# Narrow products of two weight chunks issued after the wide products of both

## The chip, the cores and the metric

The kernel runs on one core of a Trainium2 chip. The metric is the device time of one execution in microseconds (us); a profile of one execution stands beside it. Engines are called by the profile's names: PE is TensorE's matmul, PEld its weight load, DVE VectorE, ACT ScalarE, POOL GpSimd, SPq the queue that issues the DMAs.

## The reference, cut to what matters

Two blocks, 256 tokens of width 2048, all in float32. First a hybrid layer (spatial gating, a state space branch, attention over a memory, gates, an output projection), then a convolution block and a squared-ReLU MLP. Most of the time goes into products of a 256-row activation with large weights:

```
proj = rms_norm(x, pre_g) @ w_in                     # 2048 x 13312
k, v = rms_norm(mem, mem_g) @ w_k, ... @ w_v
branch = einsum('bsnc,ncd->bsnd', ys, w_branch)      # three times 1024 x 2048
out = merged @ w_out                                 # 2048 x 2048
u = h @ w_pw1 + b_pw1 ... @ w_pw2 + b_pw2            # 2048 x 4096, 2048 x 2048
h = h + square(relu(rms_norm(h) @ w_up)) @ w_down    # 2048 x 8192, 8192 x 2048
```

The attention over the memory is `softmax(q @ k.T / 16) @ v` for four heads of 256; its softmax runs while other weights are multiplied.

## The kernel before

**Chunks.** All weights come from HBM in 686 chunks of 128 x 1024 floats (512 KB). `plan()` writes out the list `STEP`: for each chunk c the job j (one output tile) and the index i of the chunk within the job. In a job of kind "W" a chunk holds eight 128 x 128 weight tiles. A job with `nch` = 2 has two chunks (K = 2048), one with `nch` = 1 has one (K = 1024). Kinds "M" and "G" and "T" are other layouts; they are not touched.

**Split in two parts.** float32 products are done as three fp32r products. Each chunk lands in `raw`; ACT copies it to the rounded `wh` (L663, `high`); DVE (in a later stretch POOL) subtracts to get the remainder `wl` (L1042, `low`), which takes the place of `raw`. Activations stand as `hi` and `lo` too. A W chunk does eight products of 512 columns (`wh` times hi and lo at once, L1854; "wide" below) and then eight of 256 columns (`wl` times hi, L1859; "narrow"), all into one PSUM bank.

**What sets the order.** Every engine runs one program in order over c. PE at step c does first the small products that other branches need at that step (the norm's sums `mean_squares` L1908 and `norm_across` L1926, `softmax` with its transposes L1972 and its products with V L1981, the state space products L1937, L1947 and L1951), then `chunk(c)`. At the end of each chunk PE raises `s_mm`. ACT's step c begins with `high(c + 3)`, which waits for `s_mm` to be c (the slot of `wh`, `WN` = 4 of them, is free); DVE's step c begins with `low(c + 3)`, which waits for that copy. What ACT and DVE do else at step c stands behind these two, since the engines don't reorder. SP issues the load of chunk c + 6 once `s_mm` is c (`RAW` = 7 slots). PE waits for `s_hi` ahead of the wide products and for `s_low_v` ahead of the narrow ones. Results leave their bank after the job's last chunk (ACT L677, DVE L1087), and three or four jobs later the bank is used again.

**The places that the prediction speaks of.** Step 9: `mean_squares(1)`, whose sums DVE and ACT turn into a diagonal matrix `dg` (L1060, L667, L1062, L1524) in their step 9, for `norm_across(1)` at PE's step 10; steps 29 and 30: the same for the memory. Steps 112 to 159: `softmax(c)`. Steps 81 to 244: the state space products `bu` and `cy`. Step 328 (`POST`): the sums after the output projection, which PE waits for.

Of the kernel before, what the change touches and what calls it, by code (L numbers as in the profile page):

```python
# [15 lines left out]
T = 256  # L16
RAW, WN = 7, 4
# [149 lines left out]
STEP, JOBS = plan()  # L167
# [27 lines left out]
LOW_V, LOW_G, HIGH = {}, {}, {}  # L195
# [105 lines left out]
def _build(nc, a, out, ctx):  # L301
    def sem(name):
        return ctx.enter_context(nc.semaphore(name))
# [4 lines left out]
    def at(name, off, n, dt=F32):  # L308
        return nc.alloc_sbuf_tensor_at(name, [128, n], dt, offset=base + off)[:, :]
# [12 lines left out]
    wl = at("wl", o_raw, RAW * CH, F32R).rearrange("p (s n) -> p s n", s=RAW)  # L322
    wh = at("wh", o_wh, WN * CH, F32R).rearrange("p (s n) -> p s n", s=WN)
# [63 lines left out]
    bank = [ctx.enter_context(nc.psum_tensor(f"bank{i}", [128, 512], F32))[:, :] for i in range(8)]  # L387
# [53 lines left out]
    s_hi, s_low_v, s_low_g, s_mm = sem("s_hi"), sem("s_low_v"), sem("s_low_g"), sem("s_mm")  # L441
# [1354 lines left out]
    def tensor(e):  # L1796
        w = Waits(e)
# [9 lines left out]
        def low_there(c):  # L1807
            if c in ON_POOL:
                w.wait_ge(s_low_g, LOW_G[c])
            else:  # L1810
                w.wait_ge(s_low_v, LOW_V[c])

        def ready(per, k):
            return k // per + 1 if per else NORMED_FOR[k]

        def chunk(c):
            j, i = STEP[c]
            pair, s_act, per, n0 = ACTS.get(j.stage, (None,) * 4)
            n0 = j.t // 4 * 16 if j.stage == "dn" else n0
            if i == 0:  # L1820
                for before in j.before:
                    if before is not None and before.kind == "W":
                        w.wait_ge(s_comb, before.comb)
                    elif before is not None:
                        w.wait_ge(s_evac, before.evac)
            if j.kind == "C":
                taps(c, j)
                return
            s, r = c % WN, c % RAW
            first_part, last_part = i == 0, i == j.nch - 1  # L1830
            if j.kind != "W":
                low_there(c)
            if j.kind == "G":
                ins = chunk_for_all(j, i, s, r, pair, s_act, per)
            elif j.kind == "M":
                for kk in range(2):
                    k = 2 * i + kk
                    w.wait_ge(s_act, n0 + k // per + 1)
                    rh = wh[:, s, kk * 512:kk * 512 + 512]
                    rl = wl[:, r, kk * 512:kk * 512 + 512]  # L1840
                    for h in range(2):
                        xh = pair.hi[:, k, h * 128:h * 128 + 128]
                        xl = pair.lo[:, k, h * 128:h * 128 + 128]
                        dst = bank[j.banks[h]]
                        e.matmul(dst, xh, rh, start=first_part and kk == 0, stop=False)  # L1845
                        e.matmul(dst, xh, rl, start=False, stop=False)  # L1846
                        ins = e.matmul(dst, xl, rh, start=False, stop=last_part and kk == 1)  # L1847
            elif j.kind == "W":
                dst = bank[j.banks[0]]
                w.wait_ge(s_hi, HIGH[c])  # L1850
                for kk in range(8):
                    k = 8 * i + kk
                    w.wait_ge(s_act, n0 + ready(per, k))
                    e.matmul(dst.rearrange("p (h t) -> p h t", h=2), wh[:, s, kk * 128:kk * 128 + 128],  # L1854
                             pair.both[:, :, k, :], start=first_part and kk == 0, stop=last_part and kk == 7,
                             skip_group_check=True)
                low_there(c)
                for kk in range(8):
                    ins = e.matmul(dst[:, 0:T], wl[:, r, kk * 128:kk * 128 + 128], pair.hi[:, 8 * i + kk, :],  # L1859
                                   start=False, stop=last_part and kk == 7, skip_group_check=True)  # L1860
            else:
                dst = bank[j.banks[0]]
                for kk in range(8):
                    k = 8 * i + kk
                    w.wait_ge(s_act, n0 + ready(per, k))
                    lh = wh[:, s, kk * 128:kk * 128 + 128]
                    ll = wl[:, r, kk * 128:kk * 128 + 128]
                    e.matmul(dst[:, 0:T], lh, pair.hi[:, k, :], start=first_part and kk == 0, stop=False)  # L1868
                    e.matmul(dst[:, 0:T], lh, pair.lo[:, k, :], start=False, stop=False)  # L1869
                    ins = e.matmul(dst[:, 0:T], ll, pair.hi[:, k, :], start=False, stop=last_part and kk == 7)  # L1870
            ins.then_inc(s_mm, 1)

        def chunk_for_all(lead, i, s, r, pair, s_act, per):


            n = len(lead.members)
            for kk in range(lead.kpc):
                k = lead.kpc * i + kk
                w.wait_ge(s_act, ready(per, k))
                for m, j in enumerate(lead.members):  # L1880
                    if k == 0:
                        for before in j.before:
                            if before is not None and before.kind == "W":
                                w.wait_ge(s_comb, before.comb)
                            elif before is not None:
                                w.wait_ge(s_evac, before.evac)
                    o = (kk * n + m) * 128
                    lh, ll = wh[:, s, o:o + 128], wl[:, r, o:o + 128]
                    a, z = k == 0 and j.col == 0, k == 15
                    if j.kind == "W":  # L1890
                        both = bank[j.banks[0]]
                        e.matmul(both.rearrange("p (h t) -> p h t", h=2), lh, pair.both[:, :, k, :], start=a, stop=z,  # L1892
                                 skip_group_check=True)
                        ins = e.matmul(both[:, 0:T], ll, pair.hi[:, k, :], start=False, stop=z, skip_group_check=True)
                        if z and j.tells:
                            ins.then_inc(s_grp, 1)
                        continue
                    e.matmul(of(j), lh, pair.hi[:, k, :], start=a, stop=False, skip_group_check=True)  # L1898
                    e.matmul(of(j), lh, pair.lo[:, k, :], start=False, stop=False, skip_group_check=True)
                    ins = e.matmul(of(j), ll, pair.hi[:, k, :], start=False, stop=z, skip_group_check=True)  # L1900
                    if z and j.tells:
                        ins.then_inc(s_grp, 1)
            return ins
# [81 lines left out]
        def taps(c, j):  # L1985


            w.wait_ge(s_raw[c % RAW], 16 * (c // RAW + 1))
            w.wait_ge(s_shift[j.idx % 3], 64 * (j.idx // 3 + 1))
            for m in range(8):  # L1990
                for g in range(4):
                    n = 32 * (8 * g + m)
                    ins = e.matmul(bank[j.banks[0]][32 * g:32 * g + 32, 0:T], raw[:, c % RAW, n:n + 32],  # L1993
                                   shifted[j.idx][:, g, 4 * m:4 * m + T], start=m == 0, stop=m == 7)
            ins.then_inc(s_mm, 1)
# [29 lines left out]
        for c in range(NC):  # L2025
# [4 lines left out]
            if c in (BIAS + 1, BIAS + 3):  # L2030
                h = (c - BIAS) // 2
# [5 lines left out]
            if Z <= c < Z + 4 * Z_STEP and (c - Z) % Z_STEP == 0:  # L2037
                i = (c - Z) // Z_STEP
# [4 lines left out]
                for g in (2 * i, 2 * i + 1):  # L2043
                    for h in range(2):
                        o = 256 * (g % 2) + 128 * h
                        ins = e.matmul(bank[7][:, o:o + 128], vn[:, h, g * 128:g * 128 + 128], sgw[:, g, :], start=True,
                                       stop=True)
# [3 lines left out]
            if S5 <= c < S5 + 32 * S5_STEP:  # L2051
                n, i = divmod(c - S5, S5_STEP)
# [39 lines left out]
            if FFN + 6 <= c < FFN + 22 and (c - FFN) % 2 == 0:  # L2092
# [5 lines left out]
                for i in range(4):  # L2098
                    ins = e.transpose(bank[4 + n % 3][:, i * 128:i * 128 + 128],
                                      Xf[:, n // 2 * 4 + i, n % 2 * 128:n % 2 * 128 + 128], ident)  # L2100
                ins.then_inc(s_tx, 1)
            chunk(c)

    with nc.Block() as block:
        @block.sync
        def _(e):
            sync(e)

        @block.gpsimd
        def _(e):  # L2110
            gpsimd(e)

        @block.scalar
        def _(e):
            scalar(e)

        @block.vector
        def _(e):
            vector(e)

        @block.tensor
        def _(e):
            tensor(e)
# [81 lines left out]
```

## Time and profile before

| | |
|---|---|
| median of 3 runs | 2039.89 us (2036.79 to 2042.66) |
| the profiled execution | 2038.79 us, of which span 2037.0 us |
| PE busy | 1997.4 us (98%) |
| DVE busy | 1526.5 us (75%) |
| ACT busy | 984.8 us (48%) |
| POOL busy | 365.6 us (18%) |
| TensorE clock granted, mean | 0.992 |

The span reaches from the first to the last instruction; 1.8 us lie around it. Matmul ends are modelled and overlap the next start, so a busy PE need not be PE at its peak; the distance between starts is what a product costs.

### The profile page before, as it was taken

The numbers are of one execution on the slowest core, as the hardware profiler recorded it, in microseconds if no ns is written. First come the engines' busy times: TensorE is split into PE (matmuls) and PEld (weight loads), VectorE is DVE, ScalarE is ACT, GpSimd is POOL, SyncE is SP. The second block draws the span as 40 slices with busy tenths as digits, with TensorE's granted clock in tenths as the row PEclk, the third lists the DMA queues.
The fourth block names the chain that finished last, engine by engine and source line by source line (L and its number), as shares of the span: only waits on it lengthen the run. The fifth ranks groups of instructions, "written<-read, shape, count | busy, mean of one in ns | idle before, by whom it ended". The sixth has DMA issues, their size and how long they took to land.

```text
span 2037.0 us, 29904 instructions
## 1 busy us (share of the span) xinstructions
PE 1997.4 (98%) x11766; PEld 1735.0 (85%) x11766; DVE 1526.5 (75%) x2398; ACT 984.8 (48%) x1451; POOL 365.6 (18%) x276
## 2 busy tenths in 40 slices
PE   8999999999899999999999999999999999999997
PEld 7888888888788888888899978888888888888886
DVE  6877889887899986688899976776467557656754
ACT  6545454444444445557543446554344444434443
POOL 0000234333333410000287744000000000000000
PEclk9999999999999999999899999999999999999999
DMA  8655555445455555565456564555665666665553
GB/s 319 216 185 177 186 186 168 163 153 167 148 176 176 164 181 191 187 228 189 142 183 209 187 193 156 190 196 190 191 193 187 195 190 190 190 195 188 188 195 134
DMA packets 107132, 379.00 MB, mean 186 GB/s; under 512 B 12016, under 2 KB 15856, under 8 KB 106864
## 3 DMA queue, kind: packets, MB, share of 16 engines
q1 hardware_dynamic: 106992, 377.09, 57.6%
q8 instruction: 93, 1.52, 0.3%
q14 instruction: 47, 0.39, 0.1%
HBM read 374.06 MB, written 2.98 MB: 185 GB/s over the span
## 4 chain that ended last, share of the span: by engine, by line
PE 81%; DVE 13%; issue 3%; ACT 2%; DMA 1%; SPq 0%; DVEq 0%; ACTq 0%
PE bank L1854 34%; PE bank L1859 17%; PE bank L1845 7%; PE bank L1846 7%; PE bank L1847 7%; DVE wl L1042 3%; DVE bank L1607 3%; ACT wh L663 1%; PE bank L1868 1%; PE bank L1870 1%; PE bank L1869 1%; PE bank L1892 1%; DVE scr L1087 1%; PE bank L1993 1%; PE bank L1898 0%
## 5 line engine op out<-in xcount | busy, mean ns | idle before, releaser
L1042 DVE TENSOR_TENSOR wl<-raw,wh 128x1024 fp32r<-128x1024 f32 x610 | 760.6, 1251 | 370.8 <-ACT wh L663 368.8
L663 ACT ACTIVATE wh<-raw 128x1024 fp32r<-128x1024 f32 x680 | 712.4, 1055 | 543.3 <-PE bank L1847 226.8
L1854 PE MATMUL bank<-Hr,wh 128*128 128x512 f32 x2304 | 581.8, 394 | 1.3 <-ACT wh L663 0.9
L1854 PEld LDWEIGHTS bank<-Hr,wh 128*128 128x128 f32 x2304 | 415.1, 189 | 81.8 <-issue 5.9
L1854 PE MATMUL bank<-Yr,wh 128*128 128x512 f32 x1280 | 326.0, 397 | 15.4 <-ACT wh L663 8.5
L1859 PEld LDWEIGHTS bank<-Hr,wl 128*128 128x128 f32 x2304 | 314.2, 190 | 22.7
L1859 PE MATMUL bank<-Hr,wl 128*128 128x256 f32 x2304 | 321.1, 282 | 0.0
L1854 PEld LDWEIGHTS bank<-Yr,wh 128*128 128x128 f32 x1280 | 231.6, 190 | 60.4 <-ACT wh L663 8.5
L606 POOL TENSOR_TENSOR wl<-raw,wh 128x1024 fp32r<-128x1024 f32 x70 | 170.0, 2437 | 350.6 <-ACT wh L663 350.6
L1845 PE MATMUL bank<-wh,Yr 128*128 128x512 f32 x576 | 224.2, 389 | 0.0
L1846 PE MATMUL bank<-wl,Yr 128*128 128x512 f32 x576 | 224.1, 389 | 0.0
L1847 PE MATMUL bank<-wh,Yr 128*128 128x512 f32 x576 | 224.1, 389 | 0.0
L1859 PEld LDWEIGHTS bank<-Yr,wl 128*128 128x128 f32 x1280 | 176.0, 192 | 12.7
L1859 PE MATMUL bank<-Yr,wl 128*128 128x256 f32 x1280 | 179.6, 283 | 0.0
L1847 PEld LDWEIGHTS bank<-wh,Yr 128*128 128x128 f32 x576 | 108.1, 188 | 22.6
L1868 PE MATMUL bank<-Hr,wh 128*128 128x256 f32 x448 | 127.4, 284 | 0.0
L1845 PEld LDWEIGHTS bank<-wh,Yr 128*128 128x128 f32 x576 | 108.2, 188 | 22.2
L1846 PEld LDWEIGHTS bank<-wl,Yr 128*128 128x128 f32 x576 | 108.2, 188 | 22.1
L1869 PE MATMUL bank<-Hr,wh 128*128 128x256 f32 x448 | 126.8, 283 | 0.0
L1870 PE MATMUL bank<-Hr,wl 128*128 128x256 f32 x448 | 126.8, 283 | 0.0
L1607 DVE SCALAR_TENSOR_TENSOR bank<-upad,cst,bank 128x256 f32<-128x256 f32 x290 | 121.7, 479 | 2.3
L621 POOL TENSOR_TENSOR wcs<-tab 128x256 f32<-128x256 f32 x32 | 39.6, 1238 | 464.8 <-DVE turned_s L1408 303.5
(334 smaller groups left out, 1925.3 us busy)
## 6 DMA issues: line engine op xcount, KB each, us to landing
raw<-in_w_up SPq DMA_DIRECT2D x128, 512.0 KB, 4.1
raw<-in_w_dn SPq DMA_DIRECT2D x128, 512.0 KB, 4.2
raw<-in_w_g SPq DMA_DIRECT2D x96, 512.0 KB, 3.5
raw<-in_w_p SPq DMA_DIRECT2D x80, 512.0 KB, 3.5
raw<-in_w_b SPq DMA_DIRECT2D x48, 512.0 KB, 3.4
raw<-in_w_out SPq DMA_DIRECT2D x32, 512.0 KB, 3.5
raw<-in_w_bx SPq DMA_DIRECT2D x16, 512.0 KB, 6.3
raw<-in_w_q SPq DMA_DIRECT2D x16, 512.0 KB, 4.1
```

The costliest lines, as they stand in the source:

```text
L606: e.tensor_tensor(wl[:, c % RAW, :], raw[:, c % RAW, :], wh[:, c % WN, :].bitcast(F32), ALU.subtract).then_inc(s_low_g, 1)
L663: e.activation(wh[:, c % WN, :], raw[:, c % RAW, :], ACT.Copy).then_inc(s_hi, 1)
L1042: e.tensor_tensor(wl[:, c % RAW, :], raw[:, c % RAW, :], wh[:, c % WN, :].bitcast(F32), ALU.subtract).then_inc(s_low_v, 1)
L1607: e.scalar_tensor_tensor(ac, pad[:, j:j + T], wj, ac, ALU.mult, ALU.add).then_inc(s_v, w.own())
L1845: e.matmul(dst, xh, rh, start=first_part and kk == 0, stop=False)
L1846: e.matmul(dst, xh, rl, start=False, stop=False)
L1847: ins = e.matmul(dst, xl, rh, start=False, stop=last_part and kk == 1)
L1854: e.matmul(dst.rearrange("p (h t) -> p h t", h=2), wh[:, s, kk * 128:kk * 128 + 128], pair.both[:, :, k, :], start=first_part and kk == 0, ...
L1859: ins = e.matmul(dst[:, 0:T], wl[:, r, kk * 128:kk * 128 + 128], pair.hi[:, 8 * i + kk, :], start=False, stop=last_part and kk == 7, skip_ ...
L1868: e.matmul(dst[:, 0:T], lh, pair.hi[:, k, :], start=first_part and kk == 0, stop=False)
L1869: e.matmul(dst[:, 0:T], lh, pair.lo[:, k, :], start=False, stop=False)
L1870: ins = e.matmul(dst[:, 0:T], ll, pair.hi[:, k, :], start=False, stop=last_part and kk == 7)
```

## The change

In a W job with two chunks that follow each other in `STEP` (184 of them: 60 of `up`, 16 each of `g0`, `g1`, `g2`, 12 of `out` and of `p2`, eight each of `q`, `k`, `au`, `ag`, `xg`, `bg`, four of `bx`), PE issues the eight wide products of the first chunk, at the next step the eight wide ones of the second, then the eight narrow ones of the first (with its `s_mm`), then those of the second (with its `s_mm`). Products of the same numbers into the same bank, as many instructions, and no other engine's program differs.

```diff
             elif j.kind == "W":
-                dst = bank[j.banks[0]]
-                w.wait_ge(s_hi, HIGH[c])
-                for kk in range(8):
...
-                low_there(c)
-                for kk in range(8):
-                    ins = e.matmul(dst[:, 0:T], wl[:, r, kk * 128:kk * 128 + 128], pair.hi[:, 8 * i + kk, :],
-                                   start=False, stop=last_part and kk == 7, skip_group_check=True)
+                wide_products(c, j, i, pair, s_act, per, n0)
+                if i == 0 and j.nch == 2 and STEP[c + 1][0] is j:
+                    return
+                if i == 1 and STEP[c - 1][0] is j:
+                    narrow_products(c - 1, j, 0, pair).then_inc(s_mm, 1)
+                ins = narrow_products(c, j, i, pair)
...
+        def wide_products(c, j, i, pair, s_act, per, n0):
+
+            w.wait_ge(s_hi, HIGH[c])
+            for kk in range(8):
+                k = 8 * i + kk
+                w.wait_ge(s_act, n0 + ready(per, k))
+                e.matmul(bank[j.banks[0]].rearrange("p (h t) -> p h t", h=2), wh[:, c % WN, kk * 128:kk * 128 + 128],
+                         pair.both[:, :, k, :], start=k == 0, stop=k == 8 * j.nch - 1, skip_group_check=True)
+
+        def narrow_products(c, j, i, pair):
+
+            low_there(c)
+            for kk in range(8):
+                ins = e.matmul(bank[j.banks[0]][:, 0:T], wl[:, c % RAW, kk * 128:kk * 128 + 128],
+                               pair.hi[:, 8 * i + kk, :], start=False, stop=8 * i + kk == 8 * j.nch - 1,
+                               skip_group_check=True)
+            return ins
```

PE at steps 8 to 10, before (L1908 is `mean_squares`, L1926 `norm_across`; `Yr` holds the activations):

```order
L1854 MATMUL bank<-Yr,wh 128x512 x8
L1859 MATMUL bank<-Yr,wl 128x256 x8
L1908 MATMUL bank<-ones,sq_71 128x1 x8
L1854 MATMUL bank<-Yr,wh 128x512 x8
L1859 MATMUL bank<-Yr,wl 128x256 x8
L1926 MATMUL bank<-dg,ones 128x256
```

The same place in the change, where L1873 is the wide product, L1880 the narrow one, L1920 `mean_squares` and L1938 `norm_across`:

```order
L1873 MATMUL bank<-Yr,wh 128x512 x8
L1920 MATMUL bank<-ones,sq_71 128x1 x8
L1873 MATMUL bank<-Yr,wh 128x512 x8
L1880 MATMUL bank<-Yr,wl 128x256 x16
L1938 MATMUL bank<-dg,ones 128x256
```

The narrow products of chunk 8, after which `s_mm` becomes 9, have moved from ahead of `mean_squares` to behind it and behind the wide products of chunk 9.

PE at steps 121 to 123, before (L1972 transposes the probabilities, L1937 is `bu`, L1981 multiplies with V):

```order
L1972 MATMUL bank<-ident,Pb_65 128x128 x2
L1937 MATMUL bank<-uT,Bs 128x256 x8
L1854 MATMUL bank<-Hr,wh 128x512 x8
L1859 MATMUL bank<-Hr,wl 128x256 x8
L1981 MATMUL bank<-pT,Vn 128x256 x2
L1854 MATMUL bank<-Hr,wh 128x512 x8
L1859 MATMUL bank<-Hr,wl 128x256 x8
L1981 MATMUL bank<-pT,Vn 128x256 x2
```

And in the change (L1984 the transposes, L1949 `bu`, L1993 the products with V):

```order
L1984 MATMUL bank<-ident,Pb_65 128x128 x2
L1949 MATMUL bank<-uT,Bs 128x256 x8
L1873 MATMUL bank<-Hr,wh 128x512 x8
L1993 MATMUL bank<-pT,Vn 128x256 x2
L1873 MATMUL bank<-Hr,wh 128x512 x8
L1880 MATMUL bank<-Hr,wl 128x256 x16
L1993 MATMUL bank<-pT,Vn 128x256 x2
```

The first product with V now follows eight wide products only; the narrow ones that stood between have moved behind it.

## Rows read from the trace of the kernel before

**Rows 1.** The page: the span, and the busy time of each engine.

```profile
span 2037.0 us, 29904 instructions
PE 1997.4 (98%) x11766; PEld 1735.0 (85%) x11766; DVE 1526.5 (75%) x2398; ACT 984.8 (48%) x1451; POOL 365.6 (18%) x276
```

**Rows 2.** Waits of PE, longest total first: total us, times, longest.

```profile
PE bank L1854 <- ACT wh L663: 9.3, 2, 8.5
PE bank L1854 <- DVE Yr L1101: 4.9, 1, 4.9
```

**Rows 3.** Timeline of PE in `up`: start, length (us), products that follow each other.

```profile
1401.35 2.00 PE L1854 MATMUL bank<-Hr,wh 128*128 128x512 f32 x8
1403.19 1.12 PE L1859 MATMUL bank<-Hr,wl 128*128 128x256 f32 x8
1404.14 2.00 PE L1854 MATMUL bank<-Hr,wh 128*128 128x512 f32 x8
```

**Rows 4.** Timeline of PE: a W chunk right behind an M chunk.

```profile
1496.80 1.98 PE L1854 MATMUL bank<-Hr,wh 128*128 128x512 f32 x8
1498.61 1.11 PE L1859 MATMUL bank<-Hr,wl 128*128 128x256 f32 x8
```

**Rows 5.** Timeline of PE in T chunks, 256 columns each, 24 products apart.

```profile
1100.03 0.28 PE L1869 MATMUL bank<-Hr,wh 128*128 128x256 f32 x1
...
1102.91 0.28 PE L1869 MATMUL bank<-Hr,wh 128*128 128x256 f32 x1
```

**Rows 6.** Timeline of steps 8 to 10, all engines, 34.8 to 40.4 us.

```profile
34.81 1.11 PE L1859 MATMUL bank<-Yr,wl 128*128 128x256 f32 x8
...
35.76 1.84 PE L1908 MATMUL bank<-ones,sq 128*128 128x1 f32 x16
...
36.02 1.06 ACT L663 ACTIVATE wh<-raw 128x1024 fp32r<-128x1024 f32 x1 [1.46 <-PE bank L1859]
...
37.47 2.09 PE L1854 MATMUL bank<-Yr,wh 128*128 128x512 f32 x8
...
38.87 0.42 DVE L1524 TENSOR_TENSOR dg<-ident,small 128x256 f32<-128x256 f32 x1
...
40.35 0.38 PE L1926 MATMUL bank<-dg,ones 128*128 128x256 f32 x1
```

**Rows 7.** Timeline of steps 29 and 30, 93.8 to 97.6 us.

```profile
93.85 0.50 PE L1908 MATMUL bank<-ones,sq 128*128 128x1 f32 x4
...
94.11 1.06 ACT L663 ACTIVATE wh<-raw 128x1024 fp32r<-128x1024 f32 x1 [1.46 <-PE bank L1859]
...
96.97 0.43 DVE L1524 TENSOR_TENSOR dg<-ident,small 128x256 f32<-128x256 f32 x1
...
97.55 0.39 PE L1926 MATMUL bank<-dg,ones 128*128 128x256 f32 x1
```

**Rows 8.** Timeline: the softmax's products at steps 116, 122, 134 and 158.

```profile
347.95 0.44 PE L1972 MATMUL bank<-ident,Pb 128*128 128x128 f32 x2
...
367.72 0.48 PE L1981 MATMUL bank<-pT,Vn 128*128 128x256 f32 x1
...
407.12 0.37 ACT L841 ACTIVATE pT<-bank 128x256 f32<-128x256 f32 x1
407.55 0.19 PEld L1981 LDWEIGHTS bank<-pT,Vn 128*128 128x128 f32 x1
...
486.67 0.48 PE L1981 MATMUL bank<-pT,Vn 128*128 128x256 f32 x1 [0.26 <-ACT pT L841]
```

**Rows 9.** Timeline at step 225, the state space products `cy(6)`.

```profile
699.06 0.64 PE L1947 MATMUL bank<-turned_s,Cs 128*32 128x256 f32 x8 [0.32 <-DVE wm L1387]
```

**Rows 10.** Timeline of DVE ahead of step 328.

```profile
989.39 1.22 DVE L1042 TENSOR_TENSOR wl<-raw,wh 128x1024 fp32r<-128x1024 f32 x1
...
991.45 0.42 DVE L1087 TENSOR_TENSOR scrB<-scrB,bank 128x256 f32<-128x256 f32 x1 [0.49 <-ACT scrB L677]
```

**Rows 11.** The stretch behind PE's 4.9 us wait at step 178: us, busy (instructions), PEclk granted.

```profile
556.00:559.00 3.00, 2.80 (x11) 2.60 (x12) 2.91 (x5) 1.43 (x3) 2.41 (x2) 0.50 0.00 0
```

More of the change, by code:

```diff
@@ L1848, in chunk @@
             elif j.kind == "W":
-                dst = bank[j.banks[0]]
-                w.wait_ge(s_hi, HIGH[c])
-                for kk in range(8):
[L1852 to L1856, printed above, removed]
-                low_there(c)
-                for kk in range(8):
-                    ins = e.matmul(dst[:, 0:T], wl[:, r, kk * 128:kk * 128 + 128], pair.hi[:, 8 * i + kk, :],
-                                   start=False, stop=last_part and kk == 7, skip_group_check=True)
+                wide_products(c, j, i, pair, s_act, per, n0)
[4 more added lines that the diff above has]
+                ins = narrow_products(c, j, i, pair)
             else:
```

## The prediction

> **What bounds the kernel now.** I read first the page, then the list of waits, then timelines of PE, step by step, at each place where it waits for another engine. The page gives PE 1997.4 of 2037.0 us [rows 1], and the longest entry in PE's list of waits is 9.3 us, the start of the program for the most part [rows 2]. So the distance between PE's starts sets the time. In `up` a W chunk takes 1.84 us for eight wide products (1401.35 to 1403.19) and 0.95 us for eight narrow ones (to 1404.14), 2.79 us together [rows 3]. PE hardly waits, but that isn't the same as having room: at some places what PE needs comes from DVE or ACT just when it asks, and the page can't show this, since a wait of nothing is not listed. The timelines around the small products show it, and there the change moves things.
>
> **What the change does to the products.** It neither adds nor removes an instruction. Of the four groups of a pair (wide, narrow, wide, narrow) it makes two. What does a switch between lengths cost? Wide products that follow narrow ones take 1.84 us [rows 3]; the eight of a chunk that follows an M chunk, so other 512 column products, take 1.81 us (1496.80 to 1498.61) [rows 4]. The second eight of a pair should take that: 0.03 us less. Against it, the eight narrow ones behind wide ones take 0.95 us [rows 3], while 24 products of 256 columns in a row take 2.88 us (1100.03 to 1102.91), 0.120 us each [rows 5], so 0.96 us for eight: 0.01 us more. Net 0.02 us a pair, times 184 pairs: **3.7 us less**. Bounds: nothing, if sixteen narrow products make the wide ones behind them slow for twice as long as eight do (no run of sixteen narrow ones ahead of wide ones stands in this trace); 5.5 us, if the 0.01 isn't paid. I take 3.7, the nearest rows.
>
> The Trainium skill (TensorE: Matmul & The Clock Gate, section "Back-to-back issue gap") gives a product's distance by its columns alone, 262 cycles for 256 and 518 for 512 at 2.4 GHz, whatever stands beside it. An estimate by that page is 8 x (262 + 518) / 2.4 GHz = 2.60 us a chunk in either order, where the row has 2.79, and the reorder would then win nothing. The rows disagree in that a wide group is 0.03 us shorter behind other wide products, and I go by the rows.
>
> **What moves.** Two times move in a pair that begins at 0. Wide products and any small product of the pair's second step come 0.95 us earlier, since the first chunk's narrow products no longer stand ahead. And `s_mm` of the first chunk comes at 1.84 + 1.84 + 0.95 = 4.63 instead of 2.79 us: 1.84 us later, plus whatever small product lies between. Behind that wait stand, on ACT, the copy `high` of the fourth chunk on and everything else of that step; on DVE the subtraction and all of that step; on SP the load of the seventh chunk on. The pair's end stays where it was, so banks and the second `s_mm` don't move. For the weights themselves this is covered: three chunks lie between release and use, some 8 us, of which the copy and the subtraction take 1.1 and 1.2 us [rows 6, 10]. For the load it is covered as well. What isn't covered are results that PE asks for one step later. I went through PE's small products in turn.
>
> **Step 9 and 10, the first norm.** Chunk 8 is the first of a pair and `mean_squares` stands at step 9. Now: chunk 8's narrow products start at 34.81, `mean_squares` at 35.76 and takes 1.71 us (to 37.47), ACT's copy starts at 36.02, 0.26 us behind the end of the narrow group; behind it come DVE's subtraction and the norm, and the matrix `dg` is done at 38.87 + 0.42 = 39.29. PE wants it at 40.35 [rows 6]: 1.06 us to spare. After: at 34.81 `mean_squares` starts, then chunk 9's wide products, then chunk 8's narrow ones: 34.81 + 1.71 + 1.84 + 0.95 = 39.31. The copy starts at 39.57, 3.55 us later than now, and the whole chain behind it with it, so `dg` is there at 42.84. PE is there at 40.35. **Wait of 2.5 us**, queued behind it on PE everything else.
>
> **Step 29 and 30, the memory's norm.** The same with half as many products, some 0.86 us. Narrow group from 93.85 - 0.95 = 92.90; its new end 92.90 + 0.86 + 1.84 + 0.95 = 96.55, the copy at 96.81 instead of 94.11, 2.70 us later. `dg` from 97.40 to 100.10, PE there at 97.55 [rows 7]. **Wait of 2.55 us.** Together 5.0 us. Bounds: nothing at the one end would need DVE to get to the norm without the subtraction ahead of it, which its order excludes; 6 us if the wide products behind a small product take longer.
>
> **Softmax and state space products.** Of the softmax's products eight (four transposes, four products with V) stand at the second step of a pair. Four of them start within 0.1 us of what they need now: the transpose at step 116 (347.95), and the product with V at steps 122, 134 and 158 (367.72, 407.55, 486.67). At step 134 ACT's copy `pT` runs from 407.12 to 407.49 and PE loads at 407.55; at step 158 PE waits already [rows 8]. PE will ask 0.95 us earlier and get it no earlier: 4 x 0.95 = **3.8 us**. The other four have 0.7 us or more to spare when moved (worked out for each from the end of its input), but half of the releases behind them come 1.84 us later; what DVE's idle time between steps doesn't take up arrives at PE. I take 2.2 us, between 0 and 4.4, half of the four. In the state space part `cy(6)` at step 225 waits already for DVE's product L1387, 0.32 us, and starts at 699.06 [rows 9]: **0.95 us** more. The others have over 2 us, or lie ahead of step 178, where PE waits 4.9 us anyway for a chain of DVE that is behind its work [rows 2].
>
> **Step 328.** The last `out` pair's first `s_mm` comes 1.84 us later. DVE's subtraction would start at 991.23 instead of 989.39; with 1.22 us for it and 0.42 us for the sum that follows, the last tile's result would start at some 992.8 instead of 991.45, less its overlap [rows 10]. PE waits for this chain now: **1.3 us**, between 0.9 and 1.84.
>
> **Sum.** -3.7 + 5.0 + 3.8 + 2.2 + 0.95 + 1.3 = +9.6 us, say +10. The profiled execution took 2038.79 us (span 2037.0), 1.1 us under the median of 2039.89. So 2048.8 for a profiled one, and **2050** against the median.
>
> **Rivals.**
> 1. *The waits shift, they don't add* (within 0.3%, 20%). A wait of 2.5 us at the start leaves DVE and ACT that much ahead, and if they are behind on their own account and not released by PE, later waits shrink. For it: at step 178 and in the steps to 224 DVE is behind, so waits there are swallowed. Against it: in the norm's steps ACT starts 0.26 us behind PE's end, so it is released by PE. If only the norms count: -3.7 + 5.0 + 1.3 = +2.6, 2042.5; this case reaches to 2046.
> 2. *Faster* (4%). The gain of a pair is larger than the rows say and the norms' chain is not in the way. From 0.065 us a pair on (12 us over 184) it outweighs my losses and 0.3%: 2033. In the rows only 0.03 is there to be had.
> 3. *The late release spreads* (slower, 14%). ACT and DVE get their work in bursts of two and then nothing for 4.6 us. If each of the 16 `g0` jobs loses 0.5 us more, that is 8 us, and if a wait of 2.5 us lets the clock fall at both norms and for longer at step 328, some 1.5 us each: 2050 + 8 + 4.5 = 2062. For it: after the 4.9 us wait at step 178 the granted clock is 0.50, that is 1.2 GHz, from 556 to 559 us [rows 11]. [...]
> 4. *The forecast* (62%), slower by 3 to 16 us.
>
> Under 0.3% (6.1 us) a measurement of this kernel can't tell from no change. Slower by more: 62 + 14 = 76%; within: 20%; faster: 4%. The range leaves out half of rival 3 and the lower half of rival 1: 2043 to 2058.
>
> **What the next profile would show.** PE's list of waits gains `norm_across` (L1938) behind DVE's `dg`, two times, 5 us in all; L1993 and L1984 wait for ACT's `pT` and DVE's `Pb`, some 4 to 6 us; the L1947 product at step 225 waits over 1 us. Sixteen wide products take 3.65 us and sixteen narrow ones 1.91 in `up`. A span under 2043 with these waits missing would say that ACT's copy isn't what stands ahead of the norm; pairs much under 5.56 us that switches cost more than the rows tell.

## The result and the profile after

| | before | after |
|---|---|---|
| median | 2040.24 us (4 runs, 2036.79 to 2042.66) | 2068.48 us (4 runs, 2065.26 to 2070.89) |
| ratio after/before, 95% interval | | 1.0139 (1.0118 to 1.0159) |
| profiled execution, its span | 2038.79, 2037.0 us | 2068.21, 2066.5 us |
| TensorE clock granted, mean | 0.992 | 0.990 |

The change makes the kernel 1.4% slower, some 28 us by the medians. The forecast was 2050 with a range of 2043 to 2058: the direction is right, the loss is nearly three times as large as forecast, and outside the range.

The page of the changed kernel, its span and busy times, beside [rows 1]:

```profile
span 2066.5 us, 29904 instructions
PE 2003.1 (97%) x11766; PEld 1738.2 (84%) x11766; DVE 1519.7 (74%) x2398; ACT 979.9 (47%) x1451; POOL 361.9 (18%) x276
```

The same instructions; PE's busy time grew by 5.7 us only, of a span that grew by 29.5. The rest is idle time. The waits of PE in the changed kernel (total us, times, longest) say for what, beside [rows 2]:

```profile
PE bank L1873 <- ACT wh L663: 9.2, 2, 8.5
PE bank L1984 <- DVE Pb L1494: 6.0, 4, 2.4
PE bank L1938 <- DVE dg L1524: 5.0, 2, 2.5
PE bank L1873 <- DVE Yr L1101: 4.9, 1, 4.9
PE bank L1993 <- ACT pT L841: 3.5, 3, 1.7
...
PE bank L1959 <- DVE wm L1387: 2.3, 2, 1.3
PE bank L1977 <- ACT pT L841: 2.1, 4, 0.5
PE bank L1993 <- ACT qT L846: 2.1, 4, 0.5
...
PE bank L1920 <- DVE keep L1502: 1.5, 1, 1.5
...
PE bank L1977 <- ACT qT L846: 0.9, 2, 0.4
...
PE bank L2058 <- ACT vn L864: 0.6, 1, 0.6
```

The entries of 9.2 and 4.9 us are old. `norm_across` (L1938) waits 5.0 us in two waits, as forecast. The softmax products (L1984, L1977, L1993) wait 14.6 us in 17 waits where one of 0.3 us stood before. Seven of the 17 are at products that the prediction had looked at; ten, 0.4 to 0.5 us each, at products that it had not. The state space product (L1959) waits at steps 165 and 225, and a sum after the output projection (L1920, `keep`) waits 1.5 us at step 328.

**Where the 29.5 us arise.** The start of each chunk's first product was read from both timelines; small differences in the stretches left out make up the remainder. The last column is how much later the changed kernel is at the end of a stretch than at its beginning.

| chunks | start of the last one, before and after | added |
|---|---|---|
| 0 to 8 | 32.97, 33.61 | +0.65 |
| 8 to 10, first norm | 40.59, 44.16 | +2.92 |
| 10 to 12 | 46.37, 51.52 | +1.58 |
| 28 to 30, memory's norm | 97.80, 105.54 | +2.76 |
| 30 to 32 | 103.58, 112.91 | +1.58 |
| 32 to 56, an ACT result (L2058) asked too early | 173.21, 183.34 | +0.80 |
| 80 to 82, `bu(0)` (L1949) asked too early | 248.65, 259.25 | +0.54 |
| 112 to 159, softmax | 491.12, 518.56 | +17.10 |
| 159 to 224, with `cy(3)` at step 165 | 695.79, 724.10 | +0.87 |
| 224 to 226, `cy(6)` | 703.83, 733.10 | +0.96 |
| 326 to 336, step 328 | 1026.29, 1055.90 | +0.80 |
| 336 to 406 | 1249.01, 1279.88 | +1.26 |
| 406 to 685, the tail | 2023.36, 2052.82 | -1.40 |

Timeline of PE at steps 8 to 10 after, the place of [rows 6], and two of its ACT and DVE rows (in brackets the idle time before a row and who ended it):

```profile
33.61 2.00 PE L1873 MATMUL bank<-Yr,wh 128*128 128x512 f32 x8
35.56 1.92 PE L1920 MATMUL bank<-ones,sq 128*128 128x1 f32 x16
37.34 2.09 PE L1873 MATMUL bank<-Yr,wh 128*128 128x512 f32 x8
39.26 2.07 PE L1880 MATMUL bank<-Yr,wl 128*128 128x256 f32 x16
...
40.47 1.06 ACT L663 ACTIVATE wh<-raw 128x1024 fp32r<-128x1024 f32 x1 [5.27 <-PE bank L1880]
...
43.33 0.42 DVE L1524 TENSOR_TENSOR dg<-ident,small 128x256 f32<-128x256 f32 x1
...
43.81 0.70 PE L1938 MATMUL bank<-dg,ones 128*128 128x256 f32 x2 [2.48 <-DVE dg L1524]
44.16 5.61 PE L1873 MATMUL bank<-Yr,wh 128*128 128x512 f32 x16
49.61 2.07 PE L1880 MATMUL bank<-Yr,wl 128*128 128x256 f32 x16
```

The narrow group begins at 39.26; its first half ends near 40.2 and raises `s_mm`, ACT's copy starts at 40.47, and `dg` is there 3.28 us later, at 43.75, for a PE that was through at 41.2. It is the chain that was forecast, and the wait is right to 0.1 us. What was not in the sum stands in the next row: sixteen wide products take 5.45 us (44.16 to 49.61). Windows of the changed kernel (us; busy us and instructions of PE, PEld, DVE, ACT, POOL; then the granted clock, the DMA share and GB/s):

```profile
42.00:43.50 1.50, 0.00 (x0) 0.00 (x0) 1.20 (x4) 0.60 (x2) 0.00 (x0) 1.00 0.91 306
45.50:47.00 1.50, 1.50 (x5) 1.22 (x4) 0.14 (x1) 0.00 (x0) 0.00 (x0) 0.50 0.57 232
48.50:50.50 2.00, 2.00 (x14) 1.79 (x13) 0.00 (x0) 0.00 (x0) 0.00 (x0) 1.00 0.00 0
107.00:109.00 2.00, 2.00 (x7) 1.54 (x6) 0.45 (x2) 0.00 (x0) 0.00 (x0) 0.50 0.00 0
```

PE is idle from 42 to 43.5, and at 45.5 to 47 the granted clock is 0.50, the 1.2 GHz level: five wide products in 1.5 us. At 48.5 it is 1.00 again. Behind the second norm (107 to 109) it is the same. Each time it costs the 1.58 us of the table.

Timeline of PE in `up` after, beside [rows 3]:

```profile
1530.85 2.08 PE L1880 MATMUL bank<-Hr,wl 128*128 128x256 f32 x16
1532.76 3.82 PE L1873 MATMUL bank<-Hr,wh 128*128 128x512 f32 x16
1536.42 2.08 PE L1880 MATMUL bank<-Hr,wl 128*128 128x256 f32 x16
```

Sixteen narrow ones 1.91 us, sixteen wide ones 3.66. Over the 163 pairs that have no small product between their chunks the median is 5.567 us, against 5.587 for the same pairs before. The reorder wins 0.020 us a pair there, 3.3 us in all. (Some recorded expectations below say 0.017 us a pair and 3.1 us; the timelines give 0.020.)

**The softmax.** PE's products that wait, of the first seven steps that have one (steps 116, 117, 122, 123, 124, 128, 129; timeline after, beside [rows 8]):

```profile
359.82 0.44 PE L1984 MATMUL bank<-ident,Pb 128*128 128x128 f32 x2 [2.45 <-DVE Pb L1494]
...
364.54 1.13 PE L1977 MATMUL bank<-KT,qT 128*128 128x256 f32 x4 [0.52 <-ACT pT L841]
...
380.58 1.13 PE L1993 MATMUL bank<-pT,Vn 128*128 128x256 f32 x4 [0.42 <-ACT pT L841]
...
385.98 1.13 PE L1993 MATMUL bank<-pT,Vn 128*128 128x256 f32 x4 [0.52 <-ACT qT L846]
...
390.35 1.13 PE L1977 MATMUL bank<-KT,qT 128*128 128x256 f32 x4 [0.44 <-ACT qT L846]
...
405.37 0.44 PE L1984 MATMUL bank<-ident,Pb 128*128 128x128 f32 x2 [1.59 <-DVE Pb L1494]
...
410.09 1.13 PE L1977 MATMUL bank<-KT,qT 128*128 128x256 f32 x4 [0.52 <-ACT pT L841]
```

Here a job of two chunks (a pair) and a job of one alternate. Steps 116, 122 and 128 are second steps of a pair: the products that the prediction went through. Steps 117, 123 and 129 are the single chunk behind the pair, and there PE waits 0.52 us each time. The timeline around step 129, all engines, shows why:

```profile
407.49 2.07 PE L1880 MATMUL bank<-Hr,wl 128*128 128x256 f32 x16
...
408.71 1.06 ACT L663 ACTIVATE wh<-raw 128x1024 fp32r<-128x1024 f32 x1 [2.60 <-PE bank L1880]
...
409.67 0.36 ACT L841 ACTIVATE pT<-bank 128x256 f32<-128x256 f32 x1
...
410.09 1.13 PE L1977 MATMUL bank<-KT,qT 128*128 128x256 f32 x4 [0.52 <-ACT pT L841]
```

`s_mm` of the pair's first chunk comes after eight of the sixteen narrow products, some 408.45. Behind it ACT does a copy of 1.06 us and then `pT`, done at 410.03. PE's cover is the other eight narrow products, 0.96 us, which end at 409.4. So it is 0.68 us late. (The list says 0.52, because it counts idle time from the modelled end of the last narrow product, 0.28 us behind its start, where the next one could start after 0.12 [rows 5]; each wait costs some 0.16 us more than listed. With 17 waits for one before that is 2.6 us more: 14.6 - 0.3 + 2.6 = 16.9 of the 17.1.)

Where a small product stands between the pair's two wide groups, the release is later still. `cy` does so at step 125 (393.25 to 395.12, 1.87 us). Timeline of ACT and DVE behind it, after:

```profile
398.29 1.06 ACT L663 ACTIVATE wh<-raw 128x1024 fp32r<-128x1024 f32 x1 [6.77 <-PE bank L1880]
...
399.38 1.23 DVE L1042 TENSOR_TENSOR wl<-raw,wh 128x1024 fp32r<-128x1024 f32 x1 [4.90 <-ACT wh L663]
```

ACT stands idle for 6.77 us and DVE for 4.90; DVE's softmax work of the next steps starts later by it, and the transpose at 405.37 (step 128) waits 1.59 us. The chain between the two was not followed row by row, but the late release alone, below, costs 1.67 us in the same stretch.

### The profile page after: what moved, and what is told of

The parts are those of the page before. It is cut to its first block, busy times and chain, and to the rows that moved or that the text cites. A ratio compares the mean times of both kernels' runs of the same rounds, so it can differ in the third digit from the quotient of the medians.

```text
span 2066.5 us, 29904 instructions
## 1 busy us (share of the span) xinstructions
PE 2003.1 (97%) x11766; PEld 1738.2 (84%) x11766; DVE 1519.7 (74%) x2398; ACT 979.9 (47%) x1451; POOL 361.9 (18%) x276
## 4 chain that ended last, share of the span: by engine, by line
PE 82%; DVE 11%; ACT 3%; issue 2%; DMA 1%; SPq 0%; DVEq 0%; ACTq 0%
PE bank L1873 35%; PE bank L1880 18%; PE bank L1846 7%; PE bank L1845 7%; PE bank L1847 7%; DVE bank L1607 3%; DVE wl L1042 3%; ACT wh L663 2%; PE bank L1862 1%; PE bank L1864 1%; PE bank L1863 1%; PE bank L1904 1%; DVE scr L1087 0%; PE bank L1963 0%; PE bank L1910 0%
## 5 line engine op out<-in xcount | busy, mean ns | idle before, releaser
L663 ACT ACTIVATE wh<-raw 128x1024 fp32r<-128x1024 f32 x680 | 704.0, 1055 | 550.0 <-PE bank L1880 228.9
L1873 PE MATMUL bank<-Hr,wh 128*128 128x512 f32 x2304 | 558.5, 393 | 0.9 <-ACT wh L663 0.7
L1873 PEld LDWEIGHTS bank<-Hr,wh 128*128 128x128 f32 x2304 | 423.0, 188 | 88.4 <-issue 5.7
L1873 PE MATMUL bank<-Yr,wh 128*128 128x512 f32 x1280 | 322.0, 399 | 15.4 <-ACT wh L663 8.5
L1880 PEld LDWEIGHTS bank<-Hr,wl 128*128 128x128 f32 x2304 | 295.9, 191 | 11.6
L1880 PE MATMUL bank<-Hr,wl 128*128 128x256 f32 x2304 | 299.4, 283 | 0.0
L1873 PEld LDWEIGHTS bank<-Yr,wh 128*128 128x128 f32 x1280 | 236.7, 191 | 63.5 <-ACT wh L663 8.5
L1880 PEld LDWEIGHTS bank<-Yr,wl 128*128 128x128 f32 x1280 | 170.5, 192 | 9.2
L1880 PE MATMUL bank<-Yr,wl 128*128 128x256 f32 x1280 | 173.1, 284 | 0.0
L1864 PE MATMUL bank<-Hr,wl 128*128 128x256 f32 x448 | 126.8, 283 | 0.0
```

Source lines behind the costliest of these rows:

```text
L663: e.activation(wh[:, c % WN, :], raw[:, c % RAW, :], ACT.Copy).then_inc(s_hi, 1)
L1873: e.matmul(bank[j.banks[0]].rearrange("p (h t) -> p h t", h=2), wh[:, c % WN, kk * 128:kk * 128 + 128], pair.both[:, :, k, :], start=k == ...
L1880: ins = e.matmul(bank[j.banks[0]][:, 0:T], wl[:, c % RAW, kk * 128:kk * 128 + 128], pair.hi[:, 8 * i + kk, :], start=False, stop=8 * i + k ...
```

## The experiments

Two theories. **A**: the release of the first chunk's slots comes late, and all of ACT's and DVE's work of that step with it. **B**: PE's demand comes 0.95 us earlier. And a question beside them: is the gain of the products real?

A list `PAIRS` of the first chunks of the 184 pairs is computed from `STEP`; `MERGED` says which of them get the new order. The others keep the old one.

**Only the two norms' pairs.**

```diff
+MERGED = {c for c in PAIRS if c in (8, 28)}
...
-                if i == 0 and j.nch == 2 and STEP[c + 1][0] is j:
+                if c in MERGED:
                     return
-                if i == 1 and STEP[c - 1][0] is j:
+                if c - 1 in MERGED:
                     narrow_products(c - 1, j, 0, pair).then_inc(s_mm, 1)
```

> Only the pairs of chunks 8 and 9 and of chunks 28 and 29 are merged, the other 182 stay as before. Theory A (the late s_mm holds back the copy on ScalarE and the norm's chain behind it): PE waits 2.5 us for dg twice, and the granted clock falls to half for some 3 us behind each wait, which costs 1.6 us each time: 8 us over before, 2048. Rival B (later waits shrink by what is waited here): under 5 us over before. A norm_across wait under 1 us would refute A.

Measured (four runs where no number is given): 2047.76 us, ratio 1.0038 (1.0023 to 1.0053), against 2038.81 before (19 runs). Chunks start 2.92 and 2.75 us later over the norms and 1.58 us later each over the two chunks behind them; the lag behind the kernel before is 9.04 us at chunk 112, and from there to chunk 178 it stays within 0.03 us of that. PE's wait at step 178 is 4.92 us, as in the kernel before (4.91). Two pairs of 184 cost a third of the loss, and nothing gives it back later: the waits add up, rival 1 is out. The window behind the first norm in this kernel:

```profile
45.50:47.00 1.50, 1.50 (x5) 1.11 (x5) 0.00 (x0) 0.00 (x0) 0.00 (x0) 0.50 0.42 172
```

**The order of before, with the late release alone.** The first chunk's narrow products stand where they stood, but its `s_mm` is raised by the last wide product of the second chunk.

```diff
-                wide_products(c, j, i, pair, s_act, per, n0)
...
+                wide_last = wide_products(c, j, i, pair, s_act, per, n0)
+                if c - 1 in MERGED:
+                    wide_last.then_inc(s_mm, 1)
                 ins = narrow_products(c, j, i, pair)
+                if c in MERGED:
+                    return
```

> The order of before (wide, narrow, wide, narrow), but in each of the 184 pairs the first s_mm is raised by the last wide product of the second chunk, 1.84 us later, which is where the change raises it. No product moves. Theory A (the late release costs): 8 us at the two norms, about 10 us in the softmax, 1 us at step 328, nothing won in the products: 18 to 24 us over before, 2058 to 2064. Rival B (what costs is that small products are asked 0.95 us earlier): within 3 us of before.

Measured: 2063.13 us, 1.0114 (1.0099 to 1.0129), inside the range of theory A. Not one product of PE has moved, and most of the loss is there. Timeline at the first norm, this kernel:

```profile
39.67 1.11 PE L1885 MATMUL bank<-Yr,wl 128*128 128x256 f32 x8
...
39.92 1.06 ACT L667 ACTIVATE wh<-raw 128x1024 fp32r<-128x1024 f32 x1 [5.10 <-PE bank L1877]
...
43.25 0.48 PE L1943 MATMUL bank<-dg,ones 128*128 128x256 f32 x1 [2.48 <-DVE dg L1528]
```

Same wait, same 2.48 us. In the softmax it loses 10.5 us. Its waits there (chunks 112 to 159):

```profile
PE bank L1998 <- ACT qT L850: 2.1, 4, 0.5
PE bank L1982 <- ACT pT L845: 2.1, 4, 0.5
PE bank L1989 <- DVE Pb L1498: 1.9, 2, 1.3
PE bank L1998 <- ACT pT L845: 1.1, 2, 0.8
PE bank L1982 <- ACT qT L850: 0.9, 2, 0.4
```

The ten waits of 0.4 to 0.5 us (first, second and last row, 5.1 us) are the changed kernel's own: they belong to the release alone.

**The new order, with the early release alone.** ACT's copy into the `wh` slot of a pair's first chunk waits for that chunk's last wide product (a new semaphore) and for its own subtraction, instead of `s_mm`. The narrow products don't read `wh`. SP still waits for `s_mm`. The copy is thus released not only earlier than in the change but 0.95 us earlier than in the kernel before; the last run below shows that this by itself wins nothing.

```diff
-            if c >= WN:
+            if c - WN in FREED:
+                w.wait_ge(s_wdone, FREED[c - WN])
+                if c - WN in ON_POOL:
+                    w.wait_ge(s_low_g, LOW_G[c - WN])
+                else:
+                    w.wait_ge(s_low_v, LOW_V[c - WN])
+            elif c >= WN:
                 w.wait_ge(s_mm, c - WN + 1)
...
+                wide_last = wide_products(c, j, i, pair, s_act, per, n0)
+                if c in MERGED:
+                    wide_last.then_inc(s_wdone, 1)
                     return
```

> The order of the change, but ScalarE's copy for the slot of a pair's first chunk no longer waits for s_mm: it waits for a signal of the last wide product of that chunk and for VectorE's subtraction of it (the last reader of the slot), so it is released 0.95 us earlier than in before. Theory A: the waits at the norms and nearly all of the softmax's go, and the products' 3.1 us remain: 2036 to 2041. Rival B (asked earlier): 4 to 8 us over before, since seven small products of the softmax and state space part still come 0.95 us earlier.

Measured: 2041.75 us (10 runs), 1.0009 (0.9999 to 1.0018). 26.7 of the 28 us are gone, with PE's order exactly that of the change. SP's loads are still released late here, so they are not what costs. The time lies 0.75 us above theory A's range and under B's 4 to 8 us more than before: both are at work, and A is much the larger. Timeline at the first norm, and the window that was at half clock:

```profile
35.17 1.06 ACT L676 ACTIVATE wh<-raw 128x1024 fp32r<-128x1024 f32 x1 [0.49 <-issue]
...
38.73 2.08 PE L1895 MATMUL bank<-Yr,wl 128*128 128x256 f32 x16
...
40.64 0.60 PE L1953 MATMUL bank<-dg,ones 128*128 128x256 f32 x2
```

```profile
45.50:47.00 1.50, 1.50 (x13) 1.46 (x13) 1.50 (x6) 0.10 (x1) 0.00 (x0) 1.00 0.57 169
```

The copy starts beside `mean_squares`, `norm_across` waits for nothing, and the clock stays at 1.00. What is left is B, and this kernel prices it: 3.11 us in the softmax (its waits are 2.3 us at L2008 and 1.1 at L1999), 0.97 at step 225, 0.54 at step 81 and 0.39 at step 165. The ten small waits of the release are not there.

**The two together in the softmax.** What each adds between the starts of the named chunks, and what the change adds (the stretches left out differ from the sum of the two by 0.08 us at most):

| chunks | late release alone | asked earlier alone | the change |
|---|---|---|---|
| 112 to 117 | +2.10 | +1.19 | +3.27 |
| 117 to 123 | +0.35 | +0.01 | +0.99 |
| 126 to 129 | +1.67 | 0.00 | +2.59 |
| 129 to 135 | +1.25 | +0.96 | +2.32 |
| 138 to 141 | +1.08 | +0.03 | +2.03 |
| 147 to 153 | +0.91 | +0.08 | +1.85 |
| 153 to 159 | +1.28 | +0.95 | +2.23 |
| 112 to 159, all | +10.50 | +3.11 | +17.10 |

At 117, 135 and 159 the two add up. At 123, 129, 141 and 153 asking earlier costs nothing by itself, since the result was ready long enough before; but the late release has eaten that room, and then 0.9 us are paid in three of these places and 0.6 in the first. That makes up the 3.5 us by which the change exceeds the two.

**Only the sixteen `g0` pairs**, whether the softmax's loss needs the waits ahead of it (`MERGED` for c from 112 to 159):

> Only the 16 pairs of g0 (steps 112 to 159, the softmax's) are merged. Theory A, now with its parts: release alone cost 10.5 us in these steps, asking earlier alone 3.1 us, both together in the change 17.1 us. Alone in the program they should cost the same 17 us, 2056. Rival C (the waits at the two norms ahead of them made DVE and ACT late or the clock different): clearly another number, under 14 or over 20 us.

Measured: 2054.55 us, 1.0077 (1.0062 to 1.0092); 15.7 us added between chunks 112 and 159, and the ten small waits are the same 5.1 us. Of the forecast 17 us 1.4 are missing. They are at chunk 117 (+1.82 for +3.27), where in the change other pairs lie ahead; which of these makes the difference was not tested. The rest of the softmax's loss needs no pair ahead of it, and rival C (under 14 or over 20 us) is out.

**Only the tail** (`c >= 330`, 72 pairs of `p2` and `up`, with no small product between a pair's chunks), whether the gain of the products is real:

> Merged are only the 72 pairs of p2 and up, behind chunk 330, where no small product stands at a pair's second step. Both theories: 0.017 us less for each pair, 1.2 us less than before in all, 2039: the timeline of a pair should be 5.57 us instead of 5.58. If the late release costs here too, the time is above that of before.

Measured: 2038.55 us (10 runs) against 2038.81, 0.9996 (0.9986 to 1.0006). The time can't tell it; the trace can: the starts move from +1.12 us at chunk 406 to -0.27 at 685, 1.39 us less over the 72 pairs, 0.019 each. The gain is there and too small for a measurement of the whole.

**Leave out the pairs in whose second step a small product stands** (162 keep the new order and the late release; of the 22 left out one, chunk 240's, has none there):

> The order of the change in the 162 pairs whose second step has no small product; the other 22 stay as before, s_mm stays the release. Theory A: no wait at the norms, nothing asked earlier; left are the late releases in those pairs of g0 that stay merged (8 of 16), so some 3 to 6 us in the softmax, and 1 to 2 us at step 328, less 2.8 us in the products: 2 to 6 us over before. If only the second step's small products mattered, it would be 2 to 3 us under before.

Measured: 2043.00 us (10 runs), 1.0016 (1.0007 to 1.0025). That is in the range of theory A. There are no norm waits and no half clock behind them; 3.2 us are lost in the softmax, where seven of the 16 pairs stay merged, and 2.45 over chunks 326 to 336, of which 1.2 are the release's (see "Step 328" below). Most of the loss hung on these 22 pairs; the release behind the other pairs still costs.

**The same 162 pairs with the early release**, a version that might beat both:

> The same 162 pairs, and the copy released by the last wide product and the subtraction, as in e3. Theory A: nothing is late and nothing asked early, left is 162 x 0.017 = 2.8 us: 2035 to 2037, 0.1 to 0.2% under before, which is at the edge of what can be measured. In the trace the starts of chunks should run ahead of before by 2.8 us at the end.

Measured: 2038.32 us against 2038.88, 0.9996 (0.9987 to 1.0005); one of its eleven executions took 6306.49 us, for a reason that nothing here shows, and is left out of the interval. The time is above the expected 2035 to 2037. Its waits in the softmax, where the changed kernel has 14.6 us:

```profile
PE bank L2019 <- ACT pT L865: 0.3, 1, 0.3
PE bank L2010 <- DVE Pb L1518: 0.2, 1, 0.2
```

The waits of the release and of the earlier demand are away, and what is left of the reorder's own gain can't be told from nothing in the time. Along the trace its starts fall from +0.61 us at chunk 8 to +0.02 at 112 and from +0.90 at 406 to -0.46 at the end, where -2.8 was expected; between chunks 336 and 406, where no kernel has a pair, it loses 1.40 us.

**The early release with the order of before**, whether it helps by itself:

> The order of before, with the early release of e3 for the first chunk of each of the 184 pairs. Theory A: PE waits for little in before, so an earlier copy wins at most the 3 us of PE's waits in g0 to g2 and step 328: 2036 to 2039. It separates e7's gain: what e8 has isn't owed to the order of the products.

Measured: 2040.82 us (10 runs), 1.0006 (0.9997 to 1.0015). Expected were 2036 to 2039. It wins nothing that can be measured: in the order of before the release was early enough.

## Why the prediction was right or wrong

Term by term, against the profiled execution (2068.21 - 2038.79 = 29.4 us):

| term | forecast | measured |
|---|---|---|
| products | -3.7 | -3.3 |
| two norm waits | +5.0 | +5.7 |
| clock behind them | 0 (in rival 3) | +3.2 |
| softmax | +6.0 | +17.2 |
| `cy(6)`, step 225 | +0.95 | +0.96 |
| step 328, the sums that wait | +1.3 | +1.2 |
| asked too early between chunks 32 and 56 | 0 | +0.9 |
| `bu(0)`, step 81, and `cy(3)`, step 165 | 0 | +1.7 |
| the rest | 0 | +1.8 |
| sum | +9.6 | +29.4 |

(Measured values for waits are from the starts, with the products' gain in those stretches taken out where it is over 0.05 us; step 328 is told below; the rest is the difference.)

**Right: what the products win.** Forecast 3.65 and 1.91 us, measured 3.66 and 1.91, and 0.020 us a pair for 0.02, though only 163 of the 184 pairs have their groups side by side. The Trainium skill (TensorE: Matmul & The Clock Gate, section "Back-to-back issue gap") gives the cycles that the prediction used for an isolated product; for a stream of weight loads and products it gives other times, also by the columns alone. By either the order is worth nothing. The runs disagree by those 0.020 us a pair, 3.3 us of 2040, and show at the same time how little is to be had from order.

**Right: the norms' chain.** 2.5 and 2.55 us forecast, 2.48 and 2.48 listed, 2.9 and 2.8 by starts (a listed wait is some 0.16 us too short; the rest was not followed). The two kernels with the late release and the one with the early release pin the cause on the release. Step 225 is right to 0.01 us, and the early release, which leaves it at 0.97, shows that it is of the other kind: asked earlier.

**Wrong, the failed step: "Softmax and state space products".** It gave 6.0 us for the softmax, and 17.2 were measured. Four things failed in it.
- It went only through products "at the second step of a pair". The late release reaches on: of the changed kernel's 17 waits ten are one step behind a pair, or at the first step of the next, where ACT's copy and result copy stand between the release and PE. They cost 5.1 us listed, 6.7 with 0.16 us more for each. The release alone shows the same ten waits.
- "The other four have 0.7 us or more to spare", of which it took "2.2 us ... half of the four" as lost. Both effects draw on the same spare time. The table of the two kernels shows that it is eaten up by the late release and then paid to the earlier demand, 0.9 us each at three of the four transposes. For the eight products together the waits listed are 9.5 us; less the 0.3 of before and with 0.16 for each of six further waits that is 10.2 us, not 6.0.
- It took the release as 1.84 us late "plus whatever small product lies between", and then priced only the 1.84. With `cy` between it is 1.84 + 1.87.
- Of the other state space products it said that they "have over 2 us, or lie ahead of step 178", whose wait would cover them. But `bu(0)` at step 81 waits 0.46 us for ACT and costs 0.54, and `cy(3)` at step 165 waits 1.07 us for DVE and costs 1.15 (0.39 with the early release). PE's wait at step 178 is 4.92 us after and was 4.91 before: it takes nothing of this back.

**Wrong: the clock.** Rival 3 named it ("some 1.5 us each") with 14%, and the sum left it out. At both norms it came: 1.58 us behind each in the change, the same in the norms' kernel, none with the early release. The length of a wait alone does not decide it: the transpose at step 116 waits 2.45 us in the changed kernel, and the clock stays at 1.00 (windows as above):

```profile
359.80:363.30 3.50, 3.48 (x22) 3.14 (x23) 3.47 (x6) 1.31 (x3) 0.00 (x0) 1.00 0.00 0
```

What tells the two cases apart, no run here shows. The Trainium skill (the same page, section "Why this matters for your kernels") warns of idle gaps between bursts, but of longer ones than these; here the windows behind the norms decide.

**Rival 3** was the right one of the four then, "each of the 16 `g0` jobs loses 0.5 us more", 2062; still 6 us short. It also had the clock low for longer at step 328, where the half clock lasts 10.2 us before and after. **Rival 1** is refuted by the norms' kernel, **rival 2** by the tail's.

**Step 328** was right: 1.3 us forecast, 1.2 measured. The sums that wait for DVE (`ones,Mf`) start 8.43 us behind chunk 326 in the change, where it was 7.20 before; with the late release alone it is 8.45, with the 162 pairs 8.43. That the whole stretch from chunk 326 to 336 grows by 0.80, 2.35 and 2.45 us in these three goes with the clock. It stands at half for 10.2 us there before and in the change, and for 13.7 us in the other two, falling while the sums still run. The kernel with only the `g0` pairs has 13.7 us too and grows by 1.05 us there, with no late release near. Windows of that kernel and of the one with the late release alone:

```profile
1009.20:1012.60 3.40, 2.17 (x11) 2.08 (x10) 0.89 (x5) 0.60 (x2) 0.00 (x0) 0.50 0.03 11
```

```profile
1013.80:1019.80 6.00, 4.46 (x21) 4.41 (x21) 2.23 (x10) 1.11 (x4) 0.00 (x0) 0.50 0.17 67
```

**The rest** of 1.8 us is not settled in full. 0.65 of it lie ahead of chunk 8, where other kernels stand between -0.24 and +0.61, and 1.26 between chunks 336 and 406, where no pair lies; there the kernel with only the norms' pairs has +1.19 too, and the others stand between -0.83 and +1.63. Against them stand the 0.4 us less than the release's 1.2 over chunks 326 to 336.

## What to carry to other kernels

When work is reordered on the engine that sets the time, ask first what its semaphores release: here a release that came 1.84 us later cost 24 us in a kernel in which no product had moved, 20 of them at the norms, in the softmax and at step 328, and moving it to the last true reader took away 26.7 of the change's 28 us. On engines that work in order, a wait for a slot that is needed only three steps later holds up results that are needed in the next; go through every product within two steps of the release, not only those that move, and count the small work between. (Another way, letting ACT and DVE do the awaited result ahead of the copy, no run here tried.) Spare time is spent once: two delays that are both covered alone may not be covered together.

## What the runs showed of the hardware that was not expected

- A wait of 2.48 us at the norms is followed by a granted clock of 0.50 although PE is busy again: from some 45.0 us in the changed kernel, where PE resumed at 43.81, and from 43.9 in the norms' kernel, where it resumed at 43.39. It costs 1.5 to 1.6 us, in three kernels at both norms (1.58, 1.58; 1.58, 1.58; 1.53, 1.53). With the listed wait gone it stays at 1.00. Not every wait of this length does it: behind the 2.45 us at step 116 it stays at 1.00 too.
- Stretches at half clock elsewhere fall differently from kernel to kernel: with those at the norms they sum to 32.7 us before, 30.7 with the early release, 37.6 in the version with 162 pairs and 45.7 with the late release alone, and between chunks 336 and 406 alone the starts move by +1.63 to -0.83 us against before. Differences of a microsecond of the whole can't be put down to an edit without its place in the trace.
- A wide product costs 227 ns in the middle of a group and 228 to 236 in its first five places behind a narrow one, whether eight or sixteen narrow ones stood ahead: 25 ns over five places. The first two narrow ones behind a wide one take 8 ns less than two later ones. The difference, 17 ns, is nearly the whole gain of the reorder, 20 ns a pair.
